# Mix stage: q, k and v of all heads as seven-product units ahead of the heads

## What is computed

```python
for l in range(DEPTH):
    x = x + 0.5 * swiglu(rmsnorm(x, norm_ffn1[l]), ffn1_gate[l], ffn1_up[l], ffn1_down[l])
    h = rmsnorm(x, norm_mix[l])
    z = h @ w_in[l]
    rq, rk, rv, rg, dq, dk, dv, g_ret, g_dil = jnp.split(z, IN_SPLITS, axis=-1)
    y_ret = retention(rq, rk, rv, rg, ret_decay_exp[l], ret_norm[l]) @ w_ret_o[l]
    y_dil = dilated_attention(dq, dk, dv, dil_q_norm[l], dil_k_norm[l], rel_bias) @ w_dil_o[l]
    gates = jax.nn.sigmoid(jnp.concatenate([g_ret, g_dil], axis=-1) + b_gate[l])
    merged = gates[..., :D_MODEL] * y_ret + gates[..., D_MODEL:] * y_dil
    x = x + merged @ w_out[l]
    x = x + 0.5 * swiglu(rmsnorm(x, norm_ffn2[l]), ffn2_gate[l], ffn2_up[l], ffn2_down[l])
```

## Time and profile before

| what | value |
|---|---|
| median of three runs | 2623.27 us (2622.72 to 2624.11) |
| span of the profiled execution | 2621.4 us |
| PE busy | 2614.9 us, 14961 matmuls |
| DVE busy | 1775.0 us |
| ACT busy | 1094.2 us |
| POOL busy | 63.3 us |
| HBM read, written | 259.75 MB, 13.28 MB |
| mix stage of layer 0 | starts about 360; heads 1 to 3 are 453.70 to 762.05; merge 762.05 to 937.00 |

### The profile page before, as it was taken

How to read it: one execution, slowest core, us unless ns; L and a number is a source line. 1 busy time by engine, 2 the same in 40 slices (tenths; PEclk the granted TensorE clock), 3 DMA queues, 4 the chain that set the end, 5 groups by cost and what they waited for, 6 DMA issues and landing times.

```text
span 2621.4 us, 38953 instructions
## 1 busy us (share of the span) xinstructions
PE 2614.9 (100%) x14961; PEld 2318.4 (88%) x14961; DVE 1775.0 (68%) x2394; ACT 1094.2 (42%) x1567; POOL 63.3 (2%) x79
## 2 busy tenths in 40 slices
PE   9999999999999999999999999999999999999999
PEld 7999988888888888999989999888888888889998
DVE  8877765574665468777788777664755645697776
ACT  5433444454543234333443344444544522343432
POOL 1111000000000000000000000000000000000000
PEclk9999999999999999999999999999999999999999
DMA  5433243233224333333223232432322343333231
GB/s 186 150 117 112 81 136 94 81 98 92 86 63 145 99 105 116 107 98 103 97 81 121 96 97 72 154 92 65 117 81 80 96 122 93 121 111 99 96 105 56
DMA packets 225756, 269.96 MB, mean 103 GB/s; under 512 B 14036, under 2 KB 182401, under 8 KB 225101
## 3 DMA queue, kind: packets, MB, share of 16 engines
q1 hardware_dynamic: 220488, 259.09, 31.4%
q0 software_dynamic: 4512, 5.04, 0.7%
q10 hardware_dynamic: 646, 4.31, 0.4%
HBM read 259.75 MB, written 13.28 MB: 104 GB/s over the span
## 4 chain that ended last, share of the span: by engine, by line
PE 99%; DVE 1%; DMA 0%; issue 0%; ACT 0%; SPq 0%; DVEq 0%; ACTq 0%
PE proj L557 25%; PE proj L559 25%; PE proj L558 25%; PE acc L558 7%; PE acc L557 7%; PE acc L559 7%; PE acc L880 1%; PE acc L819 0%; PE acc L839 0%; PE acc L802 0%; PE acc L803 0%; PE acc L829 0%; PE acc L804 0%; PE acc L828 0%; DMA raw<-in_w_in 0%
## 5 line engine op out<-in xcount | busy, mean ns | idle before, releaser
L557 PE MATMUL proj<-h_hi,ring_hi 128*128 128x256 f32 (+1 forms) x1632 | 548.8, 336 | 0.7 <-DVE h_lo L1607 0.7
L559 PE MATMUL proj<-h_hi,ring_lo 128*128 128x256 f32 (+1 forms) x1632 | 544.1, 333 | 0.0
L558 PE MATMUL proj<-h_lo,ring_hi 128*128 128x256 f32 (+1 forms) x1632 | 543.7, 333 | 0.0
L557 PE MATMUL proj<-y_hi,ring_hi 128*128 128x256 f32 (+1 forms) x1504 | 463.3, 308 | 0.0
L559 PE MATMUL proj<-y_hi,ring_lo 128*128 128x256 f32 (+1 forms) x1504 | 463.0, 308 | 0.0
L558 PE MATMUL proj<-y_lo,ring_hi 128*128 128x256 f32 (+1 forms) x1504 | 463.0, 308 | 0.0
L1143 ACT ACTIVATE ring_hi<-raw 128x1024 fp32r<-128x1024 f32 (+1 forms) x175 | 209.9, 1203 | 360.4 <-PE acc L559 194.6
L557 PEld LDWEIGHTS proj<-h_hi,ring_hi 128*128 128x128 f32 x1632 | 310.1, 190 | 32.6 <-DVE h_lo L1607 1.7
L559 PEld LDWEIGHTS proj<-h_hi,ring_lo 128*128 128x128 f32 x1632 | 309.9, 190 | 30.5
L558 PEld LDWEIGHTS proj<-h_lo,ring_hi 128*128 128x128 f32 x1632 | 310.2, 190 | 28.7
L559 PEld LDWEIGHTS proj<-y_hi,ring_lo 128*128 128x128 f32 x1504 | 287.3, 191 | 13.7
(11 more groups left out here) (277 smaller groups left out, 3663.7 us busy)
## 6 DMA issues: line engine op xcount, KB each, us to landing
raw<-in_ffn_gate SPq DMA_DIRECT2D x88, 512.0 KB, 3.6
raw<-in_ffn_up SPq DMA_DIRECT2D x88, 512.0 KB, 4.0
raw<-in_w_in SPq DMA_DIRECT2D x136, 256.0 KB, 3.6
raw<-in_w_in SPq DMA_DIRECT2D x60, 512.0 KB, 4.9
raw<-in_ffn_down SPq DMA_DIRECT2D x56, 512.0 KB, 4.4
work<-in_ffn_down SPq DMA_DIRECT2D x32, 512.0 KB, 5.7
raw<-in_w_out SPq DMA_DIRECT2D x16, 512.0 KB, 4.2
raw<-in_w_ret_o SPq DMA_DIRECT2D x12, 512.0 KB, 3.8
```

Of the source, the lines that this page charges most:

```text
L557: pe.matmul(o, s_hi, m_hi, start=start, stop=False, skip_group_check=onto)
L558: pe.matmul(o, s_hi, m_lo, start=False, stop=False, skip_group_check=onto)
L559: return pe.matmul(o, s_lo, m_hi, start=False, stop=stop, skip_group_check=onto)
```

## The change

Per layer the mix stage becomes cover, stage, heads and merge.

- **Cover** (six units of 48 matmuls): q of group 0 and rv of all heads as plain token tiles; ACT evicts them and POOL stores them to DRAM (`qkv_d`, `rv_d`). Beside it x is normalised in place of the input (`xn`), and the eight operands of the seven products are made.
- **Stage** (four units of seven products, 24 matmuls of 512 columns each): the other eight blocks of 512 columns of q, k, v, two at a time; DVE makes the four sums of weights, and the sums of results; POOL stores the results to `qkv_d`.
- **Heads** (written out, no loop; four units of two tiles): rq and rk, two pairs of gate tiles, rg. q, k, v and rv of the head come back from DRAM by SP. The gates' sigmoids are taken here and stored to `sig_d`. The dilated attention is that of the same head. A head's retention normalisation (`ret_total`, `ret_factor`, `ret_normed`, `ret_gated`, `ret_low`) moves into the next head, after the last one into the merge. The next head's q and k are squared, reduced, scaled and turned in the head.
- **Merge** (ten units): the branches in two halves, the gates reloaded from `sig_d` by SP (16 loads), `w_out` in four units as before.

The core of the diff (the loops over heads are gone, and most lines of `heads` and `merge` are new; the old ones are in the code above):

```diff
+            def stage_product(l, u, j):
+                (bank, op), n, N = ST_PRODUCTS[j], 2 * (ST_UNITS * l + u), 3 * l + 1
+                added = j >= ADDED
+                free = (st_c12, st_c21, st_u2, st_c11, st_c1, st_u3, st_c22)[j]
+                pe.wait_ge(weights_lo, piece(l, u, j) + 1 + LO_CREDIT)
...
+                for s in (0, 1):
...
+                    pe.wait_ge(free, n + s + 1)
+                    for k in range(4):
+                        c = c0 + k * SEQ
+                        last = three((PB, AB)[s][bank][:, :], mix_hi[op][:, k, s * P:(s + 1) * P], mix_lo[op][:, k, s * P:(s + 1) * P],
+                                     ring_hi[:, c:c + SEQ], ring_lo[:, c:c + SEQ], k == 0 and not added, k == 3, added)
+                    last.then_inc(tiles_done, 1)
```

```diff
-                tile_cols(u, PB[0], 0, first, between={7: [kq(4), kq(5)]} if prev else {})
...
-                tile_cols(u, PB[2], 0, between={3: [turn(0), turn(1)]} if prev else {})
-                pe.wait_ge(ret_v_ready, 4 * H + 2)
-                tile_cols(u, PB[3], 1, between={1: [turn(2), turn(3), values(0), values(1)], 5: [values(2), values(3), near_values]} if prev else {})
...
+                if n == 0:
+                    kq0 = lambda i: lambda: qk_turn(H, i, AB[2 * (i % 2)])
+                    between = ({1: [kq0(0), kq0(1)], 4: [kq0(2), kq0(3)], 7: [kq0(4), kq0(5)]}, {4: [scores(0), scores(1)]},
+                               {2: [scores(2), scores(3)]}, {4: [move]})
                 else:
+                    total = lambda: ret_total(H - 1, n - 1)
+                    between = ({0: [scores(0), scores(1)]}, {1: [total], 2: [scores(2), scores(3)]}, {4: [move]}, {})
+                between += ({0: [turn(0), turn(1)], 5: [turn(2), turn(3), values(0), values(1)]},
+                            {1: [values(2), values(3), near_values], 5: [rs(0)]},
+                            {0: [rs(1)], 1: [kq(0)], 3: [rv(0), rs(2)], 4: [kq(1)], 6: [rv(1), rs(3)], 7: [kq(2)]},
+                            {1: [rv(2)], 2: [kq(3)], 4: [rv(3)], 5: [kq(4)], 7: [kq(5)]})
```

```diff
+                    dil_exps(H, 0)
+                    dil_exps(H, 1)
+                    values_hi(H)
+                    swap_halves(H, 0, at(0).tile)
+                    dil_exps(H, 2)
+                    dil_exps(H, 3)
+                    split(at(2))
+                    swap_halves(H, 1, at(0).tile + 1)
+                dil_factors(H)
+                gate_sigmoid(H, 0, 0, at(1).tile, PB[2])
+                gate_sigmoid(H, 0, 1, at(1).tile + 1, PB[3])
+                rope_hi(H, 0)
+                rope_hi(H, 1)
+                if n + 1 < RET_HEADS:
+                    if n:
+                        act.wait_ge(ret_y, 4 * H - 2)
+                    for x in range(QK_BLOCKS):
+                        qk_square(H + 1, x)
+                dil_copy(H, 0)
+                dil_copy(H, 1)
                 split(at(3))
+                dil_copy(H, 2)
+                dil_copy(H, 3)
```

```diff
+                    for x in range(QK_BLOCKS):
+                        qk_reduce(H, x)
+                    qk_factors(H)
+                    stage_c21(l, u, 0)
+                    stage_c21(l, u, 1)
+                    qk_scale(H)
+                    stage_c12(l, u, 0)
+                    split(unit(l, HEAD_BASE))
+                    stage_c12(l, u, 1)
...
+                    dil_softmax(H, 0)
+                    dil_softmax(H, 1)
+                    split(at(1))
+                    values_lo(H)
+                    dil_softmax(H, 2)
+                    dil_softmax(H, 3)
+                    dil_spread(H, l)
+                    ret_factor(H - 1)
+                    split(at(2))
+                    dil_gather(H)
+                    rope(H, 0)
+                    ret_normed(H - 1)
                 dil_combine(H)
                 for i in range(NB):
                     dil_scale(H, i)
...
+                if n:
+                    rope(H, 1)
+                    ret_gated(H - 1)
+                rope_lo(H, 0)
+                rope_lo(H, 1)
+                if n + 1 < RET_HEADS:
+                    for x in range(QK_BLOCKS):
+                        qk_reduce(H + 1, x)
+                split(at(3))
```

```diff
+                split(at(M_R0))
+                gated_d(0)
+                ret_factor(H)
+                ret_normed(H)
+                ret_gated(H)
+                gated_d(1)
+                gated_d(2)
+                split(at(M_R1))
+                ret_low(H, RET_HEADS - 1)
+                gated_d(3)
+                split(at(M_W0))
+                gated_r(0)
+                gated_r(1)
+                merged_sum(0)
+                merged_sum(1)
+                low(0)
+                low(1)
+                gated_r(2)
+                split(at(M_D1))
+                gated_r(3)
+                merged_sum(2)
+                merged_sum(3)
                 dve.wait_ge(x_restored, 16 * (l + 1))
+                for m in range(4):
+                    add_out(0, m)
```

More of the change, by code:

```diff
@@ L81, with unit, piece, piece_tile @@
 FREE = 1
+BANK = 2
 LO_CREDIT = 2
 WARM, EARLY_SQUARES = 15, 3
[L84 to L102, removed]
+COVER_COLS = (C_DQ, C_RV, C_RV + 4 * P)
+QK_BLOCKS, BLOCKS = 6, 9
+ST_COLS = (C_DK, C_DQ + 4 * P, C_DK + 4 * P, C_DQ + 8 * P, C_DK + 8 * P, C_DV, C_DV + 4 * P, C_DV + 8 * P)
+A21, OPERANDS = 7, 8
+ST_ORDER = (S1, S3, N2, A11, A12, S4, A22, A21)
+ST_PRODUCTS = ((1, S1), (3, S3), (2, N2), (0, A11), (0, A12), (3, A22), (1, S4))
+ST_SLOTS = (2048, 0, 4096)
+TURNS = (2, 0, 1, 3, 4, 5)
+def unit(layer, i):
+    nth = i if i < ST_BASE else i - ST_UNITS * PROD
+    before = NB if i in (HEAD_BASE, HEAD_BASE + 1) else MIX_TILES[i - 1] if i else 8
+    return Unit(layer * ITEMS_LAYER + FFN_ITEMS + i, i % 2, layer * RAW_TURNS + nth // 2,
+                layer * TILES_LAYER + FFN_TILES + sum(MIX_TILES[:i]), before)
+def piece(layer, u, j):
+    return layer * ITEMS_LAYER + FFN_ITEMS + ST_BASE + PROD * u + j
+def piece_tile(layer, u, j):
+    return layer * TILES_LAYER + FFN_TILES + NB * ST_BASE + 2 * (PROD * u + j)
 def ffn_item(layer, f):
@@ L1086, in _ @@
                 ffn(l, 0)
-                heads(l, 0, False, 3 * l + 1)
-                with pe.Fori(1, RET_HEADS) as n:
-                    heads(l, n, True)
+                cover(l)
+                for u in range(ST_UNITS):
+                    for j in range(PROD):
+                        stage_product(l, u, j)
+                for n in range(RET_HEADS):
+                    heads(l, n)
                 merge(l)
@@ new lines, in cover @@
+            def cover(l):
+                split(unit(l, 1))
+                split(unit(l, 2))
+                cover_out(l, 0, 0)
+                cover_out(l, 0, 1)
+                norm_copy(3 * l + 1)
+                cover_out(l, 0, 2)
+                cover_out(l, 0, 3)
+                split(unit(l, 3))
+                mix_operand(l, 0)
+                mix_operand(l, 1)
+                split(unit(l, 4))
+                for b in range(NB):
+                    cover_out(l, 1, b)
+                mix_operand(l, 2)
+                split(unit(l, 5))
+                stage_hi(l, 0, 0)
+                stage_hi(l, 0, 1)
+                for b in range(NB):
+                    cover_out(l, 2, b)
@@ L1584, in _ @@
                 act.wait_ge(gq_ready, l + 1)
-                heads(l, 0, False, 3 * l + 1)
-                with act.Fori(1, RET_HEADS) as n:
-                    heads(l, n, True)
+                cover(l)
+                for u in range(ST_UNITS):
+                    stage(l, u)
+                for n in range(RET_HEADS):
+                    heads(l, n)
                 merge(l)
@@ L2282, in _ @@
                 ffn(l, 0, 3 * l + 1)
-                heads(l, 0, False, 3 * l + 1)
-                with dve.Fori(1, RET_HEADS) as n:
-                    heads(l, n, True)
+                cover(l)
+                for u in range(ST_UNITS):
+                    stage(l, u)
+                for n in range(RET_HEADS):
+                    heads(l, n)
                 merge(l)
```

1415 lines of the change are left out of this document (779 added, 636 removed).

## The result

The changed kernel takes **2680.2 us** (median of four runs, 2679.3 to 2682.1) against 2623.2 of the kernel before on the same chip: ratio 1.0219, interval 1.0206 to 1.0231, slower by 57 us. 2668 had been forecast, between 2620 and 2700. The profiled execution spans 2678.1 us, 56.7 more than before.

A forecast was written before the change was run, and what follows sets the result against it. PE, busy 2614.9 of 2621.4 us, was taken as the bound. 2621.4 - 49 for fewer columns + 2 x 46.8 of new PE waits = 2666 span, 2668 us median, 1.7% slower; own range 2640 to 2690, stated range 2620 to 2700.

The forecast's parts named there:

- PE's list: Matmul columns on PE: 384-column matmuls go, 512-column ones rise from 2016 to 2208 a layer; -49 us in all.
- Stage at nothing: Cover and stage: DVE's 32.1 and ACT's 15.9 us fit in a unit's 38.0 us of PE, so no cost.
- Waits, 93.6: New PE waits at the entry, in the heads and in the merge, from DVE's and ACT's lists; 46.8 us a layer.
- Turn 0 in heads 1 to 3: First turn of the probabilities: DVE reaches the scale at 29.8 us, PE is ready at 25.9; PE waits 3.8 us.
- Turn 2 in heads 1 and 2: Turn 2 needs dil_copy(0)'s bank; ACT has rope_hi(1) and six squares ahead, 9.8 us against 4.2 of PE; 5.6 us.
- move: Head 0: move waits for spread behind exponentials 2 and 3, whose softmaxes follow rope 1 and a split; 4.5 us.
- head 3's 5.4: PE waits in a layer's last head, which has no squares of a next head on ACT; 5.4 us a layer.
- rival 2: Clock falls after waits of 3.8 us and more, six a layer at 3.1 us, half taken back; 2686, chance 0.12.
- Matmuls at 0.43 us after a wait: Sign of being wrong: matmuls of 512 columns at the 1.2 GHz level's spacing, instead of 0.226, behind a PE wait.
- rival 3: DRAM reloads and stores come late, 11 us a layer more; 2690, chance 0.08.
- Rival 1: DVE and ACT keep up and only columns count; 2574, chance 0.15 whole or nearly, 0.05 halved near 2621.
- Rival 4: Stage bound by DVE, 45.6 us a unit against 38.0, 61 us over eight units; 2729, chance 0.05.

The follow-up runs named there:

- filled: Changed kernel plus 166 useless matmuls on idle banks in PE's waits at turn 0, turn 2 and head 0's move; 2664.6 us.
- root late: Changed kernel with the deferred reciprocal root's eight steps moved behind the probabilities' scaling and rope 1 on DVE in heads 1 to 3; 2681.0 us.

## Why the prediction held, and where its terms were off

The direction, the mechanism and the places were right. That the sum came within 12 us is in part luck: the waits were forecast 26 us too long, the clock was left out at 31.5, and two smaller terms were 2 to 5 us short.

1. **PE's list, -49**: -46. The 384-column spacing was mis-sized: 0.177 was read over three matmuls. In the kernel before, over 39 of them it is (381.91 - 375.14) / 39 = 0.174, which takes 2.6 us off:

```profile
375.14 0.34 PE L559 MATMUL proj<-ring_hi,h_lo 128*128 128x384 f32 x1
...
381.91 0.33 PE L559 MATMUL acc<-ring_hi,h_lo 128*128 128x384 f32 x1
```

   The 0.16 us that each wait costs beyond its idle time, 5 us in all, had no term in the sum.

2. **Stage at nothing**: right, 148.5 us without a gap with DVE at 83%.

3. **Waits, 93.6**: measured 67.6, each at its place. Turn 0 in heads 1 to 3: 3.8 forecast, 2.75 to 3.0. Turn 2 in heads 1 and 2: 5.6, 3.6. Entry to head 0: 3.2, 2.9; move: 4.5, 4.0; its turns: 3.6, 2.0 to 2.3. R0: 3.0, 2.6. add_out: 1.5, 2.3, 2.3, against 1.4, 2.0, 2.0. First score: 0.7, 0.3. Of head 3's 5.4, the items that the prediction names give 4.9. Part of the excess is the clock: a slower PE after one wait shortens the next, 4.9 to 3.6 at turn 2. The other part remains without the falls (filled): turns 0 and 2 then stand 3.0 and 4.9, still 0.8 and 0.7 under the forecast. At turn 0 half of it is PE's own work, 26.5 us from head 1's start (660.08) to its wait where 25.9 had been summed; the other half is DVE's chain, with the turn 29.25 us after that start where 29.8 had been. That lags counted once per dependent step make the second half, as the prediction said they might, is not shown.

4. **The clock, rival 2**: this is the step that failed. It was put beside the forecast, as another case at 0.12, and it belonged in the sum. Matmuls at 0.43 us after a wait had been named as a sign of being wrong, and they came. The price of 3.1 us a fall (15 slow matmuls) was high: 16 falls cost 31.5 us, 2.0 each; the five slow spacings from 690.56 to 692.84 took 2.28 us against 5 x 0.227 = 1.13. The count was low, six a layer instead of eight. The two nearly cancel: 2 x 18 = 36 before what shorter waits take back, against 31.5. Half was to be taken back, 18 net; with the fillers it was a third. So this rival had the size of the clock's cost about right, at 2686. The objection, that at the start PE came cold, falls: the waits put into the kernel before have it in mid-run. The Trainium skill's rule ("TensorE: Matmul & The Clock Gate", section "HAM oscillation — how this bites in real kernels"), that waits between bursts let the clock fall to half and each burst begin slow, holds here by the row at 691.13 and by six of six waits of 6.05 us; by four of six at 2.87 us it isn't certain for one wait of that length.

5. **Reloads late, rival 3**: no wait ended on a DMA. The rows that answer to the earlier trace rows:

```profile
qkv_d<-work POOLq DMA_DIRECT2D x72, 256.0 KB, 2.6
...
xs<-qkv_d SPq DMA_DIRECT2D x24, 512.0 KB, 5.3
...
work<-sig_d SPq DMA_DIRECT2D x32, 256.0 KB, 5.1
...
xs<-x_spill SPq DMA_DIRECT2D x2, 2048.0 KB, 7.8
```

   5.3 us for the q and k reload is the weight load's 4.9, which was taken, and not the restore's 10.1. Taking the nearer size was right.

6. **Rival 1** (only columns count, 2574) was refuted for these orders and nearly reached by others: 2596 with all of them. So the change with its orders put right is worth 27 us; the orders that it came with cost 84.

7. **Rival 4** (stage bound by DVE) fell with point 2.

## What to carry to other kernels

When a kernel with a saturated engine gets shorter, write out the other engines' lists for the new, shorter period before counting the gain: a DVE that was busy for 49.5 of head 1's 75.0 us, 66%, still made PE wait for 2.7 to 4.0 us, because one late step stood at the end of a chain. Waits that lie on one cycle have to be taken away together, since the wait of one place comes up at the next (root late); the merge's, taken away together, came up nowhere else. And price a wait of TensorE at more than its length: here 8.0 to 9.0 us for 6.05.

## What the runs showed of the hardware that was not expected

The falls of the clock are tied to the waits and cost two fifths to a half of the waits' length on top: 31.5 us beside 67.6 in the changed kernel, 15.3 beside 36.3 and 6.8 beside 17.2 with the waits put into the kernel before. Keeping PE busy with matmuls of no use through its waits is worth 15.6 us here. A wait's length alone doesn't decide: in the changed kernel 16 stretches at 0.50 stand beside 24 waits of 1.3 us and more. Behind the wait of 2.01 us that ended at 978.19 there is one, behind that of 3.52 us that ended at 2104.46 none (start:end, us, busy us as above, granted clock, DMA share, GB/s):

```profile
978.19:983.05 4.86, 4.86 (x14) 3.87 (x15) 2.96 (x5) 0.00 (x0) 0.00 (x0) 0.65 0.62 216
2104.46:2110.00 5.54, 5.54 (x38) 4.99 (x38) 3.56 (x4) 4.15 (x6) 0.00 (x0) 1.00 0.00 0
```

Why is open, and so is why two of six equal waits of 2.87 us were not followed by a fall.
